# RWKV-7 mixing: the block inverses go from VectorE and GpSimd together to GpSimd alone, in three batches

## The chip, the cores and the metric

The kernel runs on one core of a Trainium2 chip. The metric is the device time of one execution in microseconds; the median of the runs is compared.

## The reference, cut to what matters

The program is one inference step of a four-layer network over 640 tokens (512 latent, 128 context) of width 1024; each layer has a token mixer and an MLP. Layer 2's mixer is a bidirectional RWKV-7 scan, and the change lies there alone:

```python
def wkv7_scan(s0, r, w, k, v, kk, a, reverse):
    def step(s, inp):
        rt, wt, kt, vt, kkt, at = inp
        sa = jnp.einsum('bhvk,bhk->bhv', s, -kkt)
        s = s * wt[:, :, None, :] + sa[..., None] * (kkt * at)[:, :, None, :] + vt[..., None] * kt[:, :, None, :]
        return s, jnp.einsum('bhvk,bhk->bhv', s, rt)
```

The step multiplies the state by (diagonal minus rank one), so a window of 128 tokens can be done at once if a triangular 128x128 matrix is inverted for each window, head and direction. The kernel inverts its 32x32 diagonal blocks directly and gets the rest by matrix products.

## The kernel before

The 16 heads are worked in 8 pairs (KD = 8); T = 640 tokens are NW = 5 windows. The mixer has three stages.

**Preparation** (`prepare(m)` on VectorE, `diagonal`, `spread`, `key_sums`, `bonus` on TensorE, `decays`, `rates`, `exponents`, `take_blocks` on ScalarE). For each pair m and direction d VectorE makes the operands `ar0` and `bt` from `rkv`, `kk`, `e_in` and `e_neg`. SyncE's `rwkv_traffic` stores them in DRAM (`ar_d`, `bk_d`). ScalarE's `take_blocks` copies the 32x32 diagonal blocks out of PSUM and stores them in `blk_d`.

**Inversion.** 8 pairs x 2 directions x 2 heads x 5 windows x 4 = 640 blocks of 32x32, five to a partition. Forward substitution goes through 31 steps; each is a product into `inv_t` and a sum into the rows of the inverse, over (31-j)(j+1) elements a block. VectorE does three blocks of every partition, with the inverse held in PSUM (`inv_p`, which the traces call banks), and GpSimd two, with the inverse in SBUF (`inv_x0`). The input `inv_a` is loaded in two parts (`load_inverse`), the second when the last pair's blocks are stored. ScalarE copies VectorE's result to SBUF, SyncE stores both in `inv_d` and loads them back per pair and direction as `xc`.

**Scan** (`windows(m, d)` on TensorE, `scan_tile` on VectorE and ScalarE). For each pair and direction: `triangles` (masked by VectorE with copy_predicated into `at_`) and `tokens`, then the products `pairs(0)` to `pairs(5)`, of which `pairs(0)` needs `dt_`, the transposed inverse (`turn_inverse`), then states and outputs. `finish(m)` normalises the pair before on VectorE, inside the scan of pair m. SyncE loads the next pair's operands in the same loop.

Each engine runs its own list in order, and semaphores tie the lists. TensorE's first `windows` waits for `inv_copied`, since `inv_p` lies in its banks, and for `b3_landed` (operands) and `masks_landed`. GpSimd's other work is `low_part`, which splits every weight slab (L714); its list is: slabs up to the mixer, its part of the inversion, the other slabs.

Of the kernel before, what the change touches and what calls it, by code (L numbers as in the profile page):

```python
# [11 lines left out]
ALU = mybir.AluOpType  # L12
ACT = mybir.ActivationFunctionType
# [4 lines left out]
P = 128  # L18
D = 1024
KD = D // P  # L20
LAT, CTX = 512, 128
T = LAT + CTX
# [28 lines left out]
PART = ((0, HT - 2), (HT - 2, T))  # L51
INV_N = 5
INV_G = 2
INV_V = INV_N - INV_G

W = 128
NW = T // W
# [21 lines left out]
def build(nc, a, layers=(0, 1, 2, 3)):  # L79
    ctx = ExitStack()  # L80
    with ctx:
# [124 lines left out]
        kk = place("kk", [P, T])  # L206
        blocks = [place("blocks_0", [P, 2 * NW, 32]), place("blocks_1", [P, 2 * NW, 32], at=fs_at)]
        assert cursor[0] <= 229368, cursor[0]

        cursor[0] = hs_at  # L210
        inv_x = [None, place("inv_x1", [P, INV_V, 32, 32])]
        inv_t = [None, place("inv_t1", [P, INV_V * 256])]
        assert cursor[0] <= hs_at + 4 * 2 * 3 * T
        cursor[0] = hs_at + 4 * 2 * 3 * T
        inv_x[0] = place("inv_x0", [P, INV_G, 32, 32])
        inv_t[0] = place("inv_t0", [P, INV_G * 256])
        assert cursor[0] <= hs_at + 4 * 2 * 5 * T

# [6 lines left out]
        inv_at = cursor[0]  # L225
        inv_a = place("inv_a", [P, INV_N, 32, 32])
        assert cursor[0] <= ws_at
        cursor[0] = inv_at
        gt = place("gt", [P, NW, 2, P])
        xc = [place(f"xc_{d}", [P, 2 * NW, 32]) for d in range(2)]  # L230
        assert cursor[0] <= inv_at + 4 * INV_G * 1024
        cursor[0] = inv_at + 4 * INV_G * 1024
        dt_ = place("dt_", [P, 2 * NW, P])
        rhs = place("rhs", [P, NW, 2, 2, HS])
        assert cursor[0] <= ws_at
        tok = place("tok", [P, NW, 3, P], at=ws_at)
# [38 lines left out]
        pu, aux = banks[:, 0:4, :].rearrange("p (t h) n -> p t h n", t=2), banks[:, 4:8, :]  # L275
        inv_p = banks[:, 0:2 * INV_V, :].rearrange("p (q r) (s c) -> p q (r s) c", r=2, c=32)
# [79 lines left out]
        b1_done = sem("b1_done")  # L356
        inv_landed = [sem("inv_landed0"), sem("inv_landed1")]
        inv_done = sem("inv_done")
        inv_copied = sem("inv_copied")
        inv_pool = sem("inv_pool")  # L360
# [98 lines left out]
        def _(sp):  # L459
# [106 lines left out]
            def rwkv_traffic():  # L566

                sp.sem_inc(so_stored, 16)
                for j in range(2):
                    sp.wait_ge(rkv_stored[j], 16 * 2 * KD)  # L570
                inv_parts = blk_d.rearrange("(p n) -> p n", p=P)

                def load_inverse(p, q):

                    for stored in blk_stored:
                        sp.wait_ge(stored, 16 * q * KD // P)
                    sp.dma_start(inv_a[p:q, :, :, :].rearrange("p q r c -> p (q r c)"), inv_parts[p:q, :]
                                 ).then_inc(inv_landed[p > 0], 16)
# [30 lines left out]
                sp.dma_start(vd[:, :], rkv_d[0, 2]).then_inc(v_landed, 16)  # L609
                load_operands(0, 1)  # L610
                sp.dma_start(s0[:, :, :], a["s0"][0]).then_inc(s0_landed, 16)
                sp.dma_start(l2[:, 0, :, :], a["l2"][0]).then_inc(l2_landed, 16)
                inv_all = inv_d.rearrange("(p q n) -> p q n", p=P, q=INV_N)
                for q in range(INV_V):
                    sp.wait_ge(inv_copied, q + 1)
                    sp.dma_start(inv_all[:, INV_G + q, :], inv_x[1][:, q, :, :].rearrange("p r c -> p (r c)")
                                 ).then_inc(x_inv_stored, 16)
                sp.wait_ge(inv_pool, 1)
                sp.dma_start(inv_all[:, 0:INV_G, :], inv_x[0][:, :, :, :].rearrange("p q r c -> p q (r c)")
                             ).then_inc(x_inv_stored, 16)  # L620
                sp.wait_ge(x_inv_stored, 16 * (INV_V + 1))
                for d in range(2):
                    load_inverted(0, d)
                with sp.Fori(0, KD - 1) as m:
                    sp.wait_ge(vrev_ready, m + 1)
# [85 lines left out]
        def _(pool):  # L711
# [15 lines left out]

            def invert_part():

                x, t = inv_x[0][:, :, :, :], inv_t[0]  # L730
                for stored in ab_stored:
                    pool.wait_ge(stored, 32 * (KD - 1))
                pool.wait_ge(inv_landed[0], 16)
# [4 lines left out]
                pool.wait_ge(inv_landed[1], 16)  # L738
                for j in range(31):
                    n, q = 31 - j, INV_G  # L740
                    tj = t[:, 0:q * n * (j + 1)].rearrange("p (q r c) -> p q r c", q=q, r=n)
                    shape = [P, q, n, j + 1]
                    pool.tensor_tensor(tj, inv_a[:, 0:INV_G, j + 1:32, j:j + 1].to_broadcast(shape),
                                       x[:, :, j:j + 1, 0:j + 1].to_broadcast(shape), ALU.mult)
# [14 lines left out]
        def _(pe):  # L759
# [292 lines left out]
            def rwkv():  # L1052
# [185 lines left out]

                pe.wait_ge(inv_copied, INV_V)
                windows(0, 0, None)  # L1240
# [293 lines left out]
        def _(act):  # L1534
# [367 lines left out]
            def rwkv():  # L1902
# [172 lines left out]

                act.wait_ge(inv_done, 1)
                for q in range(INV_V):
                    act.activation(inv_x[1][:, q, :, :], inv_p[:, q, :, :], ACT.Copy).then_inc(inv_copied, 1)

# [172 lines left out]
        def _(dve):  # L2252
# [388 lines left out]
            def rwkv():  # L2641
# [131 lines left out]

                dve.memset(inv_p[:, :, :, :], 0.0)
                dve.drain()
                dve.memset(inv_p.rearrange("p q r c -> p q (r c)")[:, :, 0:1024:33], 1.0)
                dve.drain()
                for landed in inv_landed:
                    dve.wait_ge(landed, 16)
                for j in range(31):  # L2780
                    n = 31 - j
                    t = inv_t[1][:, 0:INV_V * n * (j + 1)].rearrange("p (q r c) -> p q r c", q=INV_V, r=n)
                    shape = [P, INV_V, n, j + 1]
                    dve.tensor_tensor(t, inv_a[:, INV_G:INV_N, j + 1:32, j:j + 1].to_broadcast(shape),
                                      inv_p[:, :, j:j + 1, 0:j + 1].to_broadcast(shape), ALU.mult)
                    dve.drain()
                    rows = inv_p[:, :, j + 1:32, 0:j + 1]
                    op = dve.tensor_tensor(rows, rows, t, ALU.add)
                    if j == 30:
                        op.then_inc(inv_done, 1)  # L2790
                    dve.drain()
# [552 lines left out]
```

## Time and profile before

| | |
|---|---|
| median of 3 runs | 3784.49 us (3779.83 to 3784.79) |
| profiled execution | 3781.54 us, span 3779.7 us |
| TensorE clock granted, mean | 0.968 |
| busy: PE, DVE, ACT, POOL | 92%, 54%, 35%, 34% |

PE is TensorE, DVE VectorE, ACT ScalarE, POOL GpSimd, SPq the queue in which SyncE issues DMAs. TensorE is busy nearly throughout; the 40 slices of the profile show two shallow stretches in the second half of layer 2's work, of which the mixer's preparation and inversion (1640 to 1850 us from the start) are the one that the change touches. Busy shares over the whole span say little about it: it is read from the order of events there.

### The profile page before, as it was taken

The page shows a single profiled execution, that of the slowest core. Times are in us where ns is not written, and L with a number is a line of the kernel's source. Part 1 is how long each engine was busy: PE and PEld are TensorE (multiplying, and loading weights), DVE is VectorE, ACT ScalarE, POOL GpSimd, SP SyncE. Part 2 cuts the span into 40 slices and gives each one's busy share as a digit, 9 for nine tenths or more (in the row PEclk, how much of TensorE's full clock was granted, in tenths as well). Part 3 has the DMA queues.
Part 4 walks back from the last instruction along what each step waited for, and adds up shares of the span by engine and source line. Part 5 has one row for each costly group of instructions (what it writes and reads, how often), then busy time and mean ns, then how long its engine had stood idle before and what let it go on. Part 6 is the DMA issues. An engine that isn't in the chain of part 4 may idle for free.

```text
span 3779.7 us, 67539 instructions
## 1 busy us (share of the span) xinstructions
PE 3473.6 (92%) x25106; PEld 3208.7 (85%) x25106; DVE 2045.8 (54%) x3535; ACT 1332.4 (35%) x2292; POOL 1295.5 (34%) x577
## 2 busy tenths in 40 slices
PE   6899999999999988974599999899999899999998
PEld 3789999998999977962488888799998776899997
DVE  7643774664266558478677676444754554331113
ACT  3343224415422255375232333343224323442223
POOL 0454334635633344301400000464335310464334
PEclk9999999999999999985799999999999999999999
DMA  7544554424455433466111111344544310343223
GB/s 268 157 127 149 195 186 142 131 83 122 133 173 176 149 107 119 143 205 217 52 56 59 43 56 35 112 127 155 185 151 134 98 34 1 101 134 95 72 72 119
DMA packets 174099, 460.36 MB, mean 122 GB/s; under 512 B 56864, under 2 KB 66528, under 8 KB 173152
## 3 DMA queue, kind: packets, MB, share of 16 engines
q1 hardware_dynamic: 145408, 438.46, 36.6%
q10 hardware_dynamic: 28512, 19.45, 1.6%
q8 instruction: 120, 1.97, 0.2%
q14 instruction: 59, 0.48, 0.0%
HBM read 419.41 MB, written 38.44 MB: 121 GB/s over the span
## 4 chain that ended last, share of the span: by engine, by line
issue 73%; POOL 16%; PE 6%; POOLq 2%; ACT 2%; DMA 1%; DVE 0%; ACTq 0%; DVEq 0%; SPq 0%
POOL ws L714 16%; PE banks L787 2%; PE banks L808 1%; PE banks L792 1%; POOLq L750 1%; POOLq L745 1%; PE banks L1117 1%; PE banks L818 0%; POOLq L722 0%; PE banks L1087 0%; PE banks L1140 0%; DMA inv_a<-blk_d 0%; ACT bt L2007 0%; DMA l<-in_l 0%; ACT L1997 0%
## 5 line engine op out<-in xcount | busy, mean ns | idle before, releaser
L714 POOL TENSOR_TENSOR ws<-wr,ws 128x1024 fp32r<-128x1024 f32 x509 | 1240.1, 2437 | 2309.6 <-ACT ws L1550 2309.3
L1550 ACT ACTIVATE ws<-wr 128x1024 fp32r<-128x1024 f32 x509 | 538.2, 1057 | 1053.6 <-PE banks L792 441.2
L787 PE MATMUL banks<-hs,ws 128*128 128x320 f32 x3712 | 564.3, 309 | 0.3 <-DVE hs L2678 0.3
L787 PEld LDWEIGHTS banks<-hs,ws 128*128 128x128 f32 x3712 | 549.3, 188 | 1.2 <-DVE hs L2678 0.9
L808 PE MATMUL banks<-hs,ws 128*128 128x320 f32 (+2 forms) x2624 | 444.9, 320 | 43.4 <-DVE hs L2316 13.7
L808 PEld LDWEIGHTS banks<-hs,ws 128*128 128x128 f32 x2624 | 403.3, 193 | 71.6 <-issue 26.2
L808 PE MATMUL banks<-fs,ws 128*128 128x320 f32 x2304 | 374.2, 312 | 12.9 <-DVE fs L3075 6.8
L2457 DVE SCALAR_TENSOR_TENSOR mjunk<-mr,banks 128x1024 f32<-128x1024 f32 x284 | 335.6, 1219 | 71.7 <-DMA mr<-in_m_slabs 48.4
L808 PEld LDWEIGHTS banks<-fs,ws 128*128 128x128 f32 x2304 | 344.1, 188 | 31.3 <-issue 12.7
L787 PE MATMUL banks<-fs,ws 128*128 128x320 f32 x2304 | 350.1, 309 | 0.0
L787 PEld LDWEIGHTS banks<-fs,ws 128*128 128x128 f32 x2304 | 340.7, 188 | 1.9 <-issue 1.9
L792 PE MATMUL banks<-hs,ws 128*128 128x320 f32 x1856 | 291.0, 309 | 0.0
L792 PEld LDWEIGHTS banks<-hs,ws 128*128 128x128 f32 x1856 | 277.0, 188 | 0.0
L818 PE MATMUL banks<-hs,ws 128*128 128x320 f32 (+2 forms) x1312 | 231.5, 318 | 1.5 <-POOL ws L714 1.5
L2178 ACT ACTIVATE relu<-banks 128x640 f32<-128x640 f32 x92 | 64.9, 706 | 426.9 <-PE banks L792 426.9
L818 PEld LDWEIGHTS banks<-hs,ws 128*128 128x128 f32 x1312 | 205.1, 194 | 11.1 <-issue 6.3
L818 PE MATMUL banks<-fs,ws 128*128 128x320 f32 x1152 | 195.2, 310 | 0.0
L792 PE MATMUL banks<-fs,ws 128*128 128x320 f32 x1152 | 180.6, 309 | 0.0
L818 PEld LDWEIGHTS banks<-fs,ws 128*128 128x128 f32 x1152 | 174.6, 188 | 3.3 <-POOL ws L714 2.1
L792 PEld LDWEIGHTS banks<-fs,ws 128*128 128x128 f32 x1152 | 171.9, 188 | 0.0
L3110 DVE TENSOR_TENSOR acc<-banks,acc 128x640 f32 x64 | 52.8, 824 | 156.4 <-PE banks L792 156.3
L2098 ACT ACTIVATE rhs<-banks 128x128 f32<-128x128 f32 x80 | 22.3, 279 | 310.2 <-PE banks L1268 310.2
(328 smaller groups left out, 4536.4 us busy)
## 6 DMA issues: line engine op xcount, KB each, us to landing
wr<-in_w_slabs SPq DMA_DIRECT2D x509, 512.0 KB, 3.6
mr<-in_m_slabs SPq DMA_DIRECT2D x167, 512.0 KB, 5.0
ar_d<-ar SPq DMA_DIRECT2D x16, 640.0 KB, 3.8
bk_d<-bt SPq DMA_DIRECT2D x16, 640.0 KB, 5.2
ar<-ar_d SPq DMA_DIRECT2D x16, 640.0 KB, 4.0
bk<-bk_d SPq DMA_DIRECT2D x16, 640.0 KB, 5.3
mx<-in_m_slabs SPq DMA_DIRECT2D x16, 512.0 KB, 6.6
rkv<-rkv_d SPq DMA_DIRECT2D x24, 320.0 KB, 5.2
```

Of the source, the lines that this page charges most:

```text
L714: pool.tensor_tensor(ws[s % 2][:, 1, :], wr[:, s % 2, :], ws[s % 2][:, 0, :].bitcast(F32), ALU.subtract).then_inc(lo_ready, 1)
L745: pool.drain()
L750: pool.drain()
L787: pe.matmul(pu[:, t % 2, h, 0:HT], ws[s % 2][:, 0, k * P:(k + 1) * P], src[:, k, part, h * HT:(h + 1) * HT], start=(k + part == 0), stop=F ...
L792: mm = pe.matmul(pu[:, t % 2, h, 0:HT], ws[s % 2][:, 1, k * P:(k + 1) * P], src[:, k, 0, h * HT:(h + 1) * HT], start=False, stop=(k == KD ...
L808: pe.matmul(pu[:, t % 2, h, 0:q - p], ws[s % 2][:, 0, k * P:(k + 1) * P], src[:, k, c, p:q], start=(k + c == 0), stop=False)
L818: mm = pe.matmul(pu[:, t % 2, h, 0:q - p], ws[s % 2][:, 1, k * P:(k + 1) * P], src[:, k, 0, p:q], start=False, stop=(k == KD - 1))
L1117: mm = pe.matmul(gates_at(m)[d][:, h, 0:HT], l2[rows, m % 2, c, :], src[rows, h * HT:(h + 1) * HT], start=True, stop=True, skip_group_chec ...
L1550: act.activation(ws[s % 2][:, 0, :], wr[:, s % 2, :], ACT.Copy).then_inc(hi_ready, 1)
L2178: act.activation(halves(relu[:, j, :]), pu[:, t % 2, :, 0:HT], ACT.Relu).then_inc(relu_ready, 1)
L2457: op = dve.scalar_tensor_tensor(mjunk[:, g, :], at, 0.5, vector[:, g, :], ALU.mult, ALU.mult, accum_out=modt[:, col, g:g + 1].rearrange("p ...
L3110: dve.tensor_tensor(out, pu[:, (t0 + j) % 2, :, 0:HT], out, ALU.add).then_inc(tile_read, 1)
```

## The change

VectorE, ScalarE and PSUM take no part in the inversion any more. GpSimd does all blocks in three batches, two blocks to a partition: pairs 0 and 1 (80 partitions), pairs 2 to 4 (120), pairs 5 to 7 (120). The first batch is loaded by SyncE at the start of its round m = 3 of the preparation and stored at the start of round m = 7. The second is loaded when the scan's first operands have been issued, and stored at round m = 1 of the scan's loop; the third is loaded there and stored at round m = 2. Operands of direction 0 are loaded only after the first batch is stored, since `bk_0`, `vd` and `vr` share its space. TensorE no longer waits for `inv_copied`. SyncE's loop over the scan is written out.

```diff
-INV_N = 5
 INV_G = 2
-INV_V = INV_N - INV_G
+INV_PAIRS = (0, 2, 5, KD)
@@ SyncE, rwkv_traffic
+                def load_blocks(i, pairs):
                     for stored in blk_stored:
-                        sp.wait_ge(stored, 16 * q * KD // P)
+                        sp.wait_ge(stored, 16 * pairs)
+                    part = batch(blk_d, i)
+                    n = part.shape[0]
+                    sp.dma_start(inv_a[i > 0][0:n, :, :, :].rearrange("p q r c -> p (q r c)"), part).then_inc(inv_landed, 16)
+                def store_inverse(i):
+                    sp.wait_ge(inv_pool, i + 1)
+                    ...
+                    sp.dma_start(part, inv_x[i > 0][0:n, :, :, :].rearrange("p q r c -> p (q r c)")).then_inc(x_inv_stored, 16)
                 for m in range(KD):
+                    if m == 3:
+                        load_blocks(0, INV_PAIRS[1])
                     if m == KD - 1:
-                        load_inverse(0, P - P // KD)
+                        store_inverse(0)
...
-                load_inverse(P - P // KD, P)
...
+                sp.wait_ge(x_inv_stored, 16)
                 load_operands(0, 0)
+                load_inverted(0, 0)
...
+                load_blocks(1, KD)
+                for m in range(KD - 1):
+                    if m == 1:
+                        store_inverse(1)
+                        load_blocks(2, KD)
+                        sp.wait_ge(x_inv_stored, 32)
+                    if m == 2:
+                        store_inverse(2)
+                        sp.wait_ge(x_inv_stored, 48)
@@ GpSimd
+            def invert(i):
+                ...
+                pool.wait_ge(inv_landed, 16 * (i + 1))
+                if i:
+                    pool.wait_ge(x_inv_stored, 16 * i)
                 (memsets and the 31 steps as before, on n partitions)
-            invert_part()
+            for i in range(3):
+                invert(i)
@@ TensorE
-                pe.wait_ge(inv_copied, INV_V)
@@ ScalarE
-                act.wait_ge(inv_done, 1)
-                for q in range(INV_V):
-                    act.activation(inv_x[1][:, q, :, :], inv_p[:, q, :, :], ACT.Copy).then_inc(inv_copied, 1)
@@ VectorE: both memsets of inv_p, the waits and the 31 steps taken out
                 dve.memset(at_[:, :, :, :, :], 0.0)
+                dve.memset(dt_[:, :, :], 0.0)
+                dve.wait_ge(blk_stored[0], 16 * KD)
                 dve.memset(sb_[:, :, :], 0.0)
-                dve.memset(dt_[:, :, :], 0.0)
```

The order of SyncE's DMAs from the end of the preparation (its last `bk_d` store) to the loads of the first inverses, before:

```order
L589 DMA bk_d<-bt_121 128x1280
L577 DMA inv_a<-blk_d 16x5120
L598 DMA mask<-in_mask 128x512
L600 DMA ar_139<-ar_d 128x1280
L602 DMA bk_141<-bk_d 128x1280
L609 DMA vd<-rkv_d 128x640
L600 DMA ar_140<-ar_d 128x1280
L602 DMA bk_142<-bk_d 128x1280
L611 DMA s_159<-in_s 128x128
L612 DMA l_115<-in_l 128x384
L616 DMA inv_d<-inv_x_135 128x1024 x3
L619 DMA inv_d<-inv_x_137 128x2048
```

And of the changed kernel at the same place:

```order
L596 DMA bk_d<-bt_121 128x1280
L604 DMA mask<-in_mask 128x512
L606 DMA ar_141<-ar_d 128x1280
L608 DMA bk_143<-bk_d 128x1280
L612 DMA xc_148<-inv_d 128x10x32
L617 DMA vd<-rkv_d 128x640
L618 DMA s_160<-in_s 128x128
L606 DMA ar_142<-ar_d 128x1280
L608 DMA bk_144<-bk_d 128x1280
L612 DMA xc_149<-inv_d 128x10x32
L621 DMA l_115<-in_l 128x384
L576 DMA inv_a_138<-blk_d 120x2048
```

No load of blocks stands ahead of the mask now, the first inverses (`xc`) are loaded among the operands, and the second batch's blocks come last.

VectorE's list from its last preparation operation to the scan's first masking, before (the inversion's 31 steps are cut to their first; names in brackets are the semaphores waited for):

```order
L2760 TENSOR_TENSOR bt_121<-bt_121,e_neg 128x640
L2774 MEMSET banks 128x3072
L2776 MEMSET banks 128x3x32
L2784 TENSOR_TENSOR inv_t_136<-inv_a,banks 128x93 [waits inv_landed1,inv_landed0]
L2788 TENSOR_TENSOR banks<-banks,inv_t_136 128x3x31
```

And after the change:

```order
L2763 TENSOR_TENSOR bt_121<-bt_121,e_neg 128x640
L2777 MEMSET at__153 128x5120
L2778 MEMSET dt__150 128x1280
L2780 MEMSET sb__155 128x512 [waits blk_stored0]
L2832 COPY_PREDICATED at__153<-mask,banks 128x1024 [waits masks_landed,tri_done]
L2832 COPY_PREDICATED at__153<-mask,banks 128x1024 [waits tri_done] x4
L2817 STREAM_TRANSPOSE dt__150<-xc_148 32x10x32 [waits xc_landed0]
```

Sixty-two operations and two memsets are gone from between the preparation and the masking.

GpSimd's list of the changed kernel where its first batch ends and its second begins:

```order
L749 TENSOR_TENSOR inv_t_137<-inv_a_135,inv_x_136 80x62
L753 TENSOR_TENSOR inv_x_136<-inv_x_136,inv_t_137 80x2x31
L741 MEMSET inv_x_139 120x2048 [waits x_inv_stored,inv_landed]
L743 MEMSET inv_x_139 120x2x32
L749 TENSOR_TENSOR inv_t_140<-inv_a_138,inv_x_139 120x62
L753 TENSOR_TENSOR inv_x_139<-inv_x_139,inv_t_140 120x2x31
```

A batch has the same 62 operations of the same length in elements as GpSimd's one part had before; there are three in a row now, all of them ahead of the next weight slab.

## Rows read from the trace of the kernel before

**Rows 1.** Chain of waits, TensorE alone, 1766 to 1850: total us, times, longest.
```profile
PE banks L1280 <- ACT inv_x L2078: 67.4, 1, 67.4
```

**Rows 2.** Timeline, all engines: start us, duration us, instruction, idle before it.
```profile
1762.10 0.46 SPq L589 DMA_DIRECT2D bk_d<-bt  x1
...
1765.02 1.81 POOL L734 MEMSET inv_x<- 128x2048 f32 x1 [132.40 <-DMA ar_d<-ar]
...
1773.64 0.36 SPq L598 DMA_DIRECT2D mask<-in_mask  x1
...
1774.53 0.42 SPq L602 DMA_DIRECT2D bk<-bk_d  x1
...
1778.31 0.33 POOL L743 TENSOR_TENSOR inv_t<-inv_a,inv_x 128x62 f32<-128x62 f32 x1 [11.16 <-DMA inv_a<-blk_d]
...
1830.25 0.80 PE L1280 MATMUL banks<-bk,ar 64*128 64x128 f32 x4 [67.41 <-ACT inv_x L2078]
...
1834.61 2.49 DVE L2846 COPY_PREDICATED at__152<-mask,banks 128x1024 f32<-128x1024 uint32 x2 [0.21 <-PE banks L1285]
...
1841.04 1.29 DVE L2846 COPY_PREDICATED at__152<-mask,banks 128x1024 f32<-128x1024 uint32 x1 [0.78 <-PE banks L1285]
...
1847.02 2.05 DVE L2831 STREAM_TRANSPOSE dt__149<-xc 32x320 f32<-32x320 f32 x4 [4.68 <-DMA xc<-inv_d]
...
1849.12 4.63 PE L1312 MATMUL banks<-dt__149,at__152 128*128 128x128 f32 x20 [8.24 <-DVE dt__149 L2831]
```

**Rows 3.** Windows: stretch, us, busy PE, PEld, DVE, ACT, POOL, clock, DMA, GB/s.
```profile
1675.00:1692.40 17.40, 11.03 (x210) 7.89 (x210) 16.83 (x22) 15.39 (x27) 0.00 (x0) 0.80 0.74 239
...
1778.00:1841.00 63.00, 9.73 (x80) 7.78 (x80) 55.20 (x69) 6.04 (x13) 53.12 (x62) 0.56 0.19 76
```

**Rows 4.** Groups by line, VectorE, 1640 to 1762: count, busy us, mean ns, idle.
```profile
L2736 DVE SCALAR_TENSOR_TENSOR kk<-rkv,pv,banks 128x640 f32<-128x640 f32 x7 | 6.1, 873 | 0.0
...
L2767 DVE TENSOR_TENSOR acc<-banks,rkv 128x640 f32<-128x640 f32 x7 | 5.5, 779 | 0.0
```

**Rows 5.** Timeline, VectorE and GpSimd, 1617 to 1625, in the preparation of pair 0.
```profile
1619.38 0.82 DVE L2759 TENSOR_TENSOR bt<-bt,e_neg 128x640 f32<-128x640 f32 x1
...
1619.56 2.90 POOL L714 TENSOR_TENSOR ws<-wr,ws 128x1024 fp32r<-128x1024 f32 x1 [5.58 <-ACT ws L1550]
1620.12 3.02 DVE L2760 TENSOR_TENSOR bt<-bt,e_neg 128x640 f32<-128x640 f32 x1
```

**Rows 6.** Lines L2457, L2846, whole span: ns min/median/max, first and last start.
```profile
L2457 DVE SCALAR_TENSOR_TENSOR mjunk<-mr,banks x284: 1215/1220/1223, 130.2 to 2858.1; 128x1024 f32<-128x1024 f32 x142
...
L2457 DVE SCALAR_TENSOR_TENSOR mjunk<-mr,silu x50: 1217/1224/3364, 9.4 to 122.2; 128x1024 f32<-128x1024 f32 x50
...
L2846 DVE COPY_PREDICATED at__152<-mask,banks x80: 1280/1305/1332, 1834.6 to 2348.0; 128x1024 f32<-128x1024 uint32 x80
```

**Rows 7.** Line L714, GpSimd's slab operation, whole span, same columns.
```profile
L714 POOL TENSOR_TENSOR ws<-wr,ws x509: 2343/2412/6407, 95.2 to 3755.6; 128x1024 fp32r<-128x1024 f32 x170
```

**Rows 8.** DMA issues at 1762.1, 1774.5 and 1840.5: KB each, us to landing.
```profile
bk_d<-bt SPq DMA_DIRECT2D x1, 640.0 KB, 9.6
...
bk<-bk_d SPq DMA_DIRECT2D x1, 640.0 KB, 7.5
...
inv_d<-inv_x SPq DMA_DIRECT2D x1, 1024.0 KB, 3.9
```

**Rows 9.** Timeline, SyncE's queue: end of the preparation's round 2, stores of round 6.
```profile
1677.84 0.91 SPq L552 DMA_DIRECT2D rkv<-rkv_d  x1
...
1745.07 1.35 SPq L589 DMA_DIRECT2D bk_d<-bt  x1
```

**Rows 10.** Timeline of the scan: SyncE's last DMA of rounds 0 and 1.
```profile
1921.21 0.34 SPq L638 DMA_DIRECT2D l<-in_l  x1
...
1987.71 0.34 SPq L638 DMA_DIRECT2D l<-in_l  x1
```

**Rows 11.** Timeline, TensorE in the scan of pair 1, behind VectorE's `finish(1)`.
```profile
1926.22 0.66 PE L1312 MATMUL banks<-rp,gt 128*128 128x64 f32 x4 [1.15 <-DVE zz L2868]
```

More of the change, by code:

```diff
@@ L206, in build @@
         kk = place("kk", [P, T])
-        blocks = [place("blocks_0", [P, 2 * NW, 32]), place("blocks_1", [P, 2 * NW, 32], at=fs_at)]
+        blocks = [place("blocks_0", [P, 2 * NW, 32]), place("blocks_1", [P, 2 * NW, 32], at=fs_at + 4 * 76 * P)]
         assert cursor[0] <= 229368, cursor[0]
[L210 to L217, printed above, removed]
+        inv_a, inv_x, inv_t = [], [], []
+        for at in (fs_at + 4 * NW * 4 * P, hs_at + 4 * 3 * 2 * T):
+            cursor[0] = at
+            inv_a.append(place(f"inv_a{len(inv_a)}", [P, INV_G, 32, 32]))
+            inv_x.append(place(f"inv_x{len(inv_x)}", [P, INV_G, 32, 32]))
+            inv_t.append(place(f"inv_t{len(inv_t)}", [P, INV_G * 256]))
+        assert cursor[0] <= hs_at + 4 * 7 * 2 * T
         cursor[0] = fs_at
@@ L225, in build @@
         inv_at = cursor[0]
[L226 to L228 removed]
         gt = place("gt", [P, NW, 2, P])
         xc = [place(f"xc_{d}", [P, 2 * NW, 32]) for d in range(2)]
[L231 to L232 removed]
+        assert cursor[0] <= inv_at + 4 * 2 * 1024
+        cursor[0] = inv_at + 4 * 2 * 1024
         dt_ = place("dt_", [P, 2 * NW, P])
         rhs = place("rhs", [P, NW, 2, 2, HS])
[L235 removed]
+        assert cursor[0] <= fs_at + 4 * 76 * P
         tok = place("tok", [P, NW, 3, P], at=ws_at)
@@ L356, in build @@
         b1_done = sem("b1_done")
[L357 to L359 removed]
+        inv_landed = sem("inv_landed")
         inv_pool = sem("inv_pool")
@@ L606, in load_inverted @@
                     sp.dma_start(xc[d][:, :, :], inv_v[2 * m + d]).then_inc(xc_landed[d], 16)
+                sp.wait_ge(x_inv_stored, 16)
                 load_operands(0, 0)
+                load_inverted(0, 0)
                 sp.dma_start(vd[:, :], rkv_d[0, 2]).then_inc(v_landed, 16)
+                sp.dma_start(s0[:, :, :], a["s0"][0]).then_inc(s0_landed, 16)
                 load_operands(0, 1)
-                sp.dma_start(s0[:, :, :], a["s0"][0]).then_inc(s0_landed, 16)
+                load_inverted(0, 1)
                 sp.dma_start(l2[:, 0, :, :], a["l2"][0]).then_inc(l2_landed, 16)
-                inv_all = inv_d.rearrange("(p q n) -> p q n", p=P, q=INV_N)
-                for q in range(INV_V):
[L615 to L624, printed above, removed]
+                load_blocks(1, KD)
[7 more added lines that the diff above has]
+                        sp.wait_ge(x_inv_stored, 48)
                     sp.wait_ge(vrev_ready, m + 1)
@@ L726, in low_parts @@
                     low_part(s1 - 1)
[L728 to L733, printed above, removed]
+            def invert(i):
+                n, q = 16 * NW * (INV_PAIRS[i + 1] - INV_PAIRS[i]) // INV_G, INV_G
+                x, t, blocks_in = inv_x[i > 0][0:n, :, :, :], inv_t[i > 0][0:n, :], inv_a[i > 0][0:n, :, :, :]
+                pool.wait_ge(inv_landed, 16 * (i + 1))
+                if i:
+                    pool.wait_ge(x_inv_stored, 16 * i)
                 pool.memset(x, 0.0)
@@ L737, in invert_part @@
                 pool.drain()
-                pool.wait_ge(inv_landed[1], 16)
                 for j in range(31):
[L740 to L743, printed above, removed]
+                    r = 31 - j
+                    tj = t[:, 0:q * r * (j + 1)].rearrange("p (q r c) -> p q r c", q=q, r=r)
+                    shape = [n, q, r, j + 1]
+                    pool.tensor_tensor(tj, blocks_in[:, :, j + 1:32, j:j + 1].to_broadcast(shape),
                                        x[:, :, j:j + 1, 0:j + 1].to_broadcast(shape), ALU.mult)
@@ L2074, in rwkv @@
                 take_blocks(KD - 1, 1)
-                act.wait_ge(inv_done, 1)
-                for q in range(INV_V):
-                    act.activation(inv_x[1][:, q, :, :], inv_p[:, q, :, :], ACT.Copy).then_inc(inv_copied, 1)
                 def norm_squares_of(m):
@@ L2772, in rwkv @@
                     prepare(m)
[L2774 to L2791, printed above, removed]
                 dve.memset(at_[:, :, :, :, :], 0.0)
+                dve.memset(dt_[:, :, :], 0.0)
+                dve.wait_ge(blk_stored[0], 16 * KD)
                 dve.memset(sb_[:, :, :], 0.0)
-                dve.memset(dt_[:, :, :], 0.0)
                 dve.drain()
```

11 lines of the change are left out of this document (6 added, 5 removed).

## The prediction

> **What bounds the kernel now.** I read the chain of waits of TensorE first, since it is busy 92% of the span: its one long gap near the change is 67.4 us at the first product of the scan (L1280), ended by ScalarE's copy of the inverse out of PSUM [rows 1]. The timeline then gives the order there. VectorE's last preparation operation ends with the last stores (issued 1762.1), the block load that needs them lands late, both inversions start at 1778.3, the scan's first product runs at 1830.25, and its product with the inverse, L1312, at 1849.12, behind GpSimd's share and the way through DRAM [rows 2]. From 1849.12 on the scan runs its own chain. So what counts is when L1312 can start, against the end of the preparation.
>
> The windows say who sets that end: VectorE is busy 16.83 of 17.4 us, the period of one pair, TensorE 11.03, ScalarE 15.39, GpSimd 0 [rows 3]. The preparation is VectorE's.
>
> **What the change takes out.** Let D be the time that the preparation becomes longer. The last `bk_d` store, issued at 1762.1, lands 9.6 us later, at 1771.7 [rows 2, 8]; behind that SyncE may issue the mask, with no block load in between. From the mask's issue (1773.64) to the landing of `bk_0` (1774.53 + 7.5 = 1782.0) it took 8.4 us [rows 2, 8]. The first product then runs at 1771.7 + 8.4 = 1780.1 + D. VectorE's memsets lie ahead of that. From 1830.25 to the end of the fifth masking (1842.33) were 12.1 us, of which some 2.2 because a memset held VectorE until 1834.61; four transposes add 2.05 [rows 2]. L1312 so starts at 1780.1 + 12.0 + D = 1792.1 + D, where 1849.12 stood. The gain is 57.0 - D, less what the scan loses. `xc` is loaded among the operands and should be there before the masking ends.
>
> **D, the price of the first batch.** Its load follows round 2 of SyncE (1678.8, [rows 9]) and lands some 5 us later, an estimate between the 3.9 and 7.5 us of [rows 8]; after a memset of 1.81 [rows 2] the 62 operations start near 1686.6, in pair 3. [...] Beside the inversion of before this cost VectorE nothing, but there it read one operand from PSUM. In the preparation most of its operations read two SBUF tensors. What happens then stands at 1620.12: a product of 0.82 us beside a slab operation of GpSimd takes 3.02, 2.20 more [rows 5]. GpSimd waited for the operation in progress (2.90 instead of its median 2.41, [rows 7]), then held VectorE for all of its own time but 0.2 us. Line L2457 separates the cases: with `silu` in SBUF as second input one of 50 took 3364 ns instead of 1224, with PSUM as second input none of 284 exceeds 1223; the masking, with one SBUF input, keeps to 1280 to 1332, five of its 80 beside the inversion [rows 6].
>
> So each of the 62 holds VectorE for its time less 0.2: 53.1 - 62 x 0.2 = 40.7 us. Not all of VectorE's time is exposed: per pair L2736 (0.87) and L2767 (0.78), which read PSUM, and some 0.6 us of waits and a tiny reciprocal, 2.3 of 17.4 or 13% [rows 3, 4]. D = 0.87 x 40.7 = 35 us. The bounds: the 0.2 is seen on operations of 2.4 us and may not exist for small ones, then D = 0.87 x 53.1 = 46; below, nothing excludes that the short ones slip between VectorE's, D near 0.
>
> [...]
>
> Does the batch end in time? Each GpSimd operation also waits for VectorE's current one, about 0.4 us for 87% of 62, 22 us; 1686.6 + 62 (1778.31 to 1840.5 before, [rows 2]) + 22 = 1771. Round 7, which waits for it, comes at 1746.4 + 35 = 1781 [rows 9]. It fits by 10 us; the store lands 3.9 later [rows 8].
>
> **Batches two and three.** The second is issued last of the scan's loads, at about 1777 + D. Ten transfers are ahead of it; I put its landing at 1789 + D and its end at 1853 + D. SyncE asks for it after its last DMA of round 0, 1921.5 - 57 = 1864.5 + D [rows 10]. The third then lands near 1870 + D, ends near 1935 + D, and is asked for at 1988.1 - 57 = 1931 + D. SyncE waits 4 us and 4 for the store. Queued behind it are `vd` of pair 3 and then that pair's operands, which wait for an output of pair 2, due some 18 us later (half of the 66.5 us between the two rows less what round 2 has spent): free. Without that cover a microsecond there would be one of TensorE.
>
> VectorE's exposed operations in the scan are few: by the code, in direction 0 of a pair, the copy of `vd`, two scalings, one tiny product, and four of `finish`, eight in all; the products for `zz` and the maskings read PSUM. `finish` is on the path already, by 1.15 us [rows 11]. In the old times the two batches lie at 1848 to 1911 and 1928 to 1993. The end of pair 1's `finish`, just ahead of 1926, falls in the pause; pair 2's, 66.5 later, in the third batch. Eight operations at half of 0.66 each is 2.7; I take 3 us. Bounds: 0, and two pairs with the full 0.66 eight times, 10.6.
>
> **The sum.** 57.0 - 35 - 3 = 19. The profiled execution (span 3779.7, time 3781.54) would come to 3762.5, the median of 3784.5 to 3765.5.
>
> **Rivals.** *No exclusion for these short operations.* D near 0, gain 54 to 57, 3729. For it: GpSimd's operations are a third as long as the one observed. Against: every observation of the pair. 0.10. *Partly*: D between 5 and 25, gain 25 to 49, 3748: 0.12.
>
> *GpSimd keeps VectorE out for longer than it works.* If the lock were kept through the drain between two operations, the batch would hold VectorE for its whole 62.2 us: D = 62, 57 - 62 - 3 = -8, 3792, slower. It decides from D = 54 on. For it: a pause of only 0.15 us between GpSimd's operations. Against: VectorE went on 0.2 us before the end of the slab operation. 0.08. [...]
>
> *The first batch is starved.* If VectorE's unbroken chain kept GpSimd waiting, D would be 0, but most of the batch would run after 1762, round 7 of SyncE would hold the last stores for some 50 us, and L1312 would start near 1845: within 0.2%, 3781. Against: GpSimd got in after one operation at 1619.56. 0.05.
>
> **The numbers.** The forecast with D from 28 to 42 and a scan loss of 0 to 8 has 0.53: its own range is 3757 to 3778. A change of 0.2% (7.6 us) is what a measurement of this kernel can tell from none. Faster: 0.10 + 0.12 + 0.53, and 0.03 of the rule's case, 0.78. Within: the rule's other 0.09 and the starved case, less a little, 0.13. Slower: 0.09. The range leaves out the case with no exclusion and the slow one: 3740 to 3783.
>
> **What would show it.** In the changed kernel's trace: the pair's period in the preparation grows from 17.4 to 28 or so while GpSimd works and falls back after; VectorE's L2763 and like lines have medians near 0.82 but maxima of 1.5 to 2; the last `bk_d` store is near 1797; L1312 of the scan near 1827; GpSimd's gap between batches lies in pair 1. Wrong would be: durations of VectorE untouched (first rival), a preparation that ends after 1816, a wait of SyncE for `inv_pool` that delays the last stores, or pairs of the scan that take over 70 us each.

## The result, and the profile after

The changed kernel takes **3761.98 us** (median of 5 runs, 3759.67 to 3769.98) against 3784.46 (5 runs of the kernel before beside them): a ratio of **0.9949**, 95% interval 0.9934 to 0.9963. The ratio is estimated from all the runs; that of the two medians is 0.9941. By the medians the kernel is 22.5 us faster, by the means of the same runs (3763.48 and 3782.95) 19.5; 19 were forecast. The profiled execution took 3761.98 us, and its page begins:

```profile
span 3760.2 us, 67495 instructions
...
PE 3480.1 (93%) x25106; PEld 3213.0 (85%) x25106; DVE 2037.3 (54%) x3471; ACT 1329.7 (35%) x2289; POOL 1434.9 (38%) x705
```

The span is 19.5 us shorter. The chain of waits of TensorE in the changed kernel, 1640 to 1850 us (total, times, longest), answers to [rows 1]:

```profile
PE banks L1116 <- DVE ta L2752: 36.4, 4, 12.3
...
PE banks L1286 <- DMA bk<-bk_d: 12.8, 1, 12.8
...
PE banks L1318 <- DVE dt__150 L2817: 3.4, 1, 3.4
```

The wait of 67.4 us for the inverse is gone. TensorE now waits 36.4 us for VectorE in the preparation, at a line where it waited 5.0 before, and 12.8 us for the last operands on their way through DRAM. The timeline of the changed kernel, all engines, gives the same places as [rows 2], and operations of GpSimd's first and second batch:

```profile
1707.55 1.35 POOL L749 TENSOR_TENSOR inv_t<-inv_a,inv_x 80x414 f32<-80x414 f32 x1
...
1709.50 1.64 DVE L2761 TENSOR_TENSOR ar<-rkv,e_in 128x640 f32<-128x640 f32 x1
1710.60 1.40 POOL L749 TENSOR_TENSOR inv_t<-inv_a,inv_x 80x440 f32<-80x440 f32 x1
1711.06 1.62 DVE L2762 TENSOR_TENSOR bt<-bt,e_neg 128x640 f32<-128x640 f32 x1
...
1714.34 0.76 DVE L2770 TENSOR_TENSOR acc<-banks,rkv 128x640 f32<-128x640 f32 x1
...
1777.80 0.90 SPq L583 DMA_DIRECT2D inv_d<-inv_x  x1
...
1794.36 0.79 SPq L596 DMA_DIRECT2D bk_d<-bt  x1
1801.06 0.33 SPq L604 DMA_DIRECT2D mask<-in_mask  x1
...
1807.95 0.80 PE L1286 MATMUL banks<-bk,ar 64*128 64x128 f32 x4 [12.84 <-DMA bk<-bk_d]
...
1821.95 3.48 PE L1318 MATMUL banks<-dt__150,at__153 128*128 128x128 f32 x20 [3.44 <-DVE dt__150 L2817]
...
1835.11 0.96 POOL L749 TENSOR_TENSOR inv_t<-inv_a,inv_x 120x414 f32<-120x414 f32 x1
```

The reader is to see two engines that hold each other up. GpSimd's operation on 414 elements takes 0.96 us beside the scan and 1.35 beside the preparation; VectorE's products, 0.82 alone [rows 5], take 1.62 to 1.64; and the one that reads PSUM keeps its 0.76. The last `bk_d` store is issued at 1794.36 instead of 1762.10: **D is 32.3 us** (32.1 when each is counted from the first `bk_d` store of its own run, as below). The product with the inverse (L1318 now) starts at 1821.95 instead of 1849.12, 27.2 us earlier.

The windows of the changed kernel, one pair of the preparation in each (columns as in [rows 3]):

```profile
1693.40:1720.97 27.57, 14.13 (x215) 9.65 (x218) 27.16 (x22) 19.39 (x33) 25.02 (x19) 0.63 0.52 158
1720.97:1752.00 31.03, 14.05 (x210) 9.60 (x210) 30.72 (x21) 15.47 (x26) 28.47 (x19) 0.50 0.42 134
1752.00:1776.90 24.90, 12.60 (x210) 8.57 (x210) 24.50 (x22) 13.86 (x23) 22.20 (x20) 0.60 0.40 139
1776.90:1794.36 17.46, 4.81 (x197) 3.27 (x198) 16.67 (x21) 5.03 (x15) 0.21 (x1) 0.56 0.64 205
```

Pairs 3 to 5 take 10.2, 13.6 and 7.5 us more than the 17.4 of [rows 3], and pair 6, beside which GpSimd has finished, 17.46. VectorE counts as busy throughout (27.16 of 27.57 us in pair 3): the time that it is kept out stands inside its operations.

The scan loses time in one pair only. A round is the time from one last DMA of SyncE's loop to the next, one pair of the scan. SyncE's queue in the timeline of the changed kernel, last DMA of rounds 0 to 3, against [rows 10]:

```profile
1893.34 0.33 SPq L644 DMA_DIRECT2D l<-in_l  x1
...
1959.92 0.33 SPq L644 DMA_DIRECT2D l<-in_l  x1
...
2031.45 0.33 SPq L644 DMA_DIRECT2D l<-in_l  x1
...
2097.95 0.33 SPq L644 DMA_DIRECT2D l<-in_l  x1
```

The rounds are 66.6, **71.5** and 66.5 us; the second batch costs nothing, the third 5.0. Where, VectorE and TensorE show in the same timeline, in pair 1 (between the batches) and in pair 2 (beside the third):

```profile
1887.85 0.48 DVE L2839 COPY vr<-vd 128x640 f32<-128x640 f32 x1
1888.24 0.51 DVE L2844 TENSOR_SCALAR sb__155<-s,ewin 64x64 f32<-64x64 f32 x2
1888.79 0.16 DVE L2846 TENSOR_TENSOR ecm<-ewin 128x3 f32 x1
...
1898.49 0.66 PE L1318 MATMUL banks<-rp,gt 128*128 128x64 f32 x4 [1.17 <-DVE zz L2854]
...
1954.44 0.69 DVE L2839 COPY vr<-vd 128x640 f32<-128x640 f32 x1
...
1955.06 1.17 DVE L2844 TENSOR_SCALAR sb__155<-s,ewin 64x64 f32<-64x64 f32 x2
...
1956.26 0.84 DVE L2846 TENSOR_TENSOR ecm<-ewin 128x3 f32 x1
...
1967.06 1.11 PE L1318 MATMUL banks<-rp,gt 128*128 128x64 f32 x4 [3.15 <-DVE zz L2854]
...
1967.96 7.25 PE L1318 MATMUL banks<-zz,gt 128*128 128x128 f32 x40
```

From the copy to `zz` VectorE needs 2.0 us longer in pair 2, and TensorE waits 3.15 instead of 1.17. The 40 matmuls behind that take 7.25 us, 4.63 in the kernel before, and the first four 1.11 instead of 0.66: 2.0 + 2.6 + 0.45 is the 5.0. The windows of the changed kernel around them show what happened to the clock:

```profile
1957.00:1967.90 10.90, 7.75 (x60) 7.24 (x60) 9.82 (x11) 3.20 (x10) 9.34 (x12) 0.94 0.06 18
1967.96:1975.20 7.24, 7.24 (x42) 7.24 (x43) 3.94 (x11) 0.00 (x0) 2.25 (x6) 0.62 0.46 114
```

The granted clock was 0.62 over those 7.24 us, behind a wait of 3.15 us: 0.50 over the first 3.00 of them and 0.71 over the last 4.20. From 1975.2 to 1985.0 it is 1.00 again, and over the same 40 matmuls of pair 1, behind the wait of 1.17 us, it was 1.00 too.

### The profile page after: what moved, and what is told of

Read it like the earlier page. It is cut to its first block, busy times and chain, and to the rows that moved or that the text cites. A ratio compares the mean times of both kernels' runs of the same rounds, so it can differ in the third digit from the quotient of the medians.

```text
span 3760.2 us, 67495 instructions
## 1 busy us (share of the span) xinstructions
PE 3480.1 (93%) x25106; PEld 3213.0 (85%) x25106; DVE 2037.3 (54%) x3471; ACT 1329.7 (35%) x2289; POOL 1434.9 (38%) x705
## 4 chain that ended last, share of the span: by engine, by line
issue 69%; POOL 16%; PE 7%; DVE 3%; POOLq 2%; DMA 1%; DVEq 1%; ACT 1%; ACTq 0%; SPq 0%
POOL ws L720 16%; PE banks L794 2%; PE banks L815 1%; PE banks L799 1%; PE banks L1318 1%; POOLq L756 1%; POOLq L751 1%; PE banks L825 0%; POOLq L728 0%; PE banks L1094 0%; PE banks L1124 0%; DVE ar L2761 0%; DVE bt L2763 0%; PE banks L1147 0%; DVE ar L2759 0%
## 5 line engine op out<-in xcount | busy, mean ns | idle before, releaser
L815 PEld LDWEIGHTS banks<-fs,ws 128*128 128x128 f32 x2304 | 344.1, 188 | 31.8 <-issue 12.7
```

What stands on the lines that cost most here:

```text
L815: pe.matmul(pu[:, t % 2, h, 0:q - p], ws[s % 2][:, 0, k * P:(k + 1) * P], src[:, k, c, p:q], start=(k + c == 0), stop=False)
```

## The experiments

All are made from the changed kernel. Ratios are to runs of the kernel before that stood beside them: 3782.67 us for c0, e1, e2 and e4, 3786.11 for e3, e5 and e6, 3784.11 for e7, e8 and e9. The start of the preparation shifts by some us from run to run, so D is counted from the run's own first `bk_d` store (1640.77 in the kernel before).

**The changed kernel again**, for the spread.

> The changed kernel once more, as the measure for the other runs of this call. Both theories: 3762 us, within 5; pairs 3 to 6 of the preparation 27 to 31 us each, round 2 of the scan 71.5 us between SyncE's last DMAs against 66.5 of the others. If that 5 us was a chance event of one execution, it is missing here.

Measured: 3761.26 us (3756.86 to 3763.29), ratio 0.9943 (0.9927 to 0.996). D is 32.1, the round of pair 2 71.7 us. Both losses repeat.

**e1: the first batch behind the preparation.** The transfer of the blocks moves behind round 7:

```diff
-                    if m == 3:
-                        load_blocks(0, INV_PAIRS[1])
-                    if m == KD - 1:
-                        store_inverse(0)
...
                 sp.wait_ge(b1_done, KD)
+                load_blocks(0, KD)
                 sp.dma_start(mask[:, :], a["mask"]).then_inc(masks_landed, 16)
+                store_inverse(0)
```

> The first batch's blocks are loaded only when the preparation is over, and the scan's operands after the batch, so that GpSimd is idle in the preparation. Theory (GpSimd's operations keep VectorE out): all pairs of the preparation are back to 17.4 us, its last store is issued at 1762, 32 us sooner, and the 62 operations last 62 us as in the kernel before; the batch with its load, store and the operands behind it stands on the path, so the scan's product with the first inverse comes near 1866 instead of 1822 and the time is about 3762 + 44 = 3806. Rival (the preparation is longer because of the new places of the buffers or the DMA traffic): the pairs stay at 27 to 31 us, and the time is near 3838.

Measured: 3806.04 us (3802.58 to 3807.06), ratio **1.0065** (1.0049 to 1.0082). The last `bk_d` store is at 1762.05, D = 0, and the product with the inverse starts at 1862.7, 13.6 us later than before. TensorE's chain of waits in e1, 1640 to 1900 us:

```profile
PE banks L1284 <- DMA bk<-bk_d: 85.9, 1, 85.9
```

Placing the batch beside the preparation is worth 45 us (3806.04 - 3761.26). Without that the change is a loss. The batch on GpSimd alone ends at 1838.40, about where the shared inversion ended (1840.45), but the first operands use its space and are issued only at 1842.61, behind its store; in the kernel before they had been issued at 1774.5. What GpSimd alone would cost with the operands in a place of their own was not tried.

**e2: the first batch only writes.** Its 62 operations become 62 `memset` of the inverse's own space, two for each step, which read nothing and are somewhat shorter (0.68 us on average instead of 0.86). It leaves out the inverses of pairs 0 and 1.

```diff
+                    if i == 0:
+                        flat = x.rearrange("p q r c -> p (q r c)")[:, 0:2 * q * r * (j + 1)]
+                        pool.memset(flat, 0.0)
+                        pool.drain()
+                        op = pool.memset(flat, 0.0)
...
```

> In the first batch each product and each sum is replaced by a memset of the inverse's own space with twice the elements (the first two pairs' inverses are thus not computed), so GpSimd is busy about as long but reads nothing from SBUF. Theory (the second SBUF input of VectorE and a read of GpSimd exclude each other): VectorE's preparation operations stay at 0.82 us, the last store is issued near 1762, the product with the inverse comes near 1790, the time is about 3762 - 32 = 3730. Rival (any GpSimd operation on SBUF keeps VectorE out, or the time goes to its being busy as such): the pairs are stretched by 8 to 14 us each as in the changed kernel, 3755 to 3762.

Measured: 3727.48 us (3724.63 to 3733.81), ratio **0.9854** (0.9838 to 0.9871). GpSimd's groups by line in e2, 1689 to 1790 us, and, by line over the whole span, VectorE's product that is L2763 in the changed kernel:

```profile
L751 POOL MEMSET inv_x<- 80x124 f32 (+15 forms) x31 | 21.1, 681 | 3.6
L753 POOL MEMSET inv_x<- 80x124 f32 (+15 forms) x31 | 21.1, 681 | 3.6
```

```profile
L2772 DVE TENSOR_TENSOR bt<-bt,e_neg x16: 814/817/2992, 1621.1 to 1763.1; 128x640 f32<-128x640 f32 x16
```

42.2 us of GpSimd's work lie beside the preparation and VectorE's median stays at 817 ns; the maximum of 2992 is the slab operation of [rows 5]. The preparation ends as in the kernel before. So D is not the price of a busy GpSimd, of its queue, its semaphores or SyncE's moved transfers; it is the price of what GpSimd reads. The round of pair 2, beside whose scan the third batch still reads, stays at 71.8.

**e3: the first batch on 16 partitions** instead of 80. It leaves out the inverses of four fifths of the first batch's blocks.

```diff
+                if i == 0:
+                    n, x, t, blocks_in = 16, x[0:16], t[0:16, :], blocks_in[0:16]
```

> The 62 operations of the first batch run on 16 partitions instead of 80 (the other blocks of pairs 0 and 1 stay uninverted). Theory (VectorE is kept out for the time of an operation, whatever it moves): nothing changes, 3761 us, pairs 3 to 6 at 27 to 31 us. Rival (the two share bandwidth, so that a fifth of the data costs a fifth): the preparation is 25 us shorter, 3736 us.

Measured: 3763.54 us (3762.35 to 3765.36), ratio 0.9942 (0.9927 to 0.9957), as the changed kernel. GpSimd and VectorE in e3's timeline:

```profile
1712.10 1.35 POOL L751 TENSOR_TENSOR inv_t<-inv_a,inv_x 16x414 f32<-16x414 f32 x1
...
1715.62 1.62 DVE L2764 TENSOR_TENSOR bt<-bt,e_neg 128x640 f32<-128x640 f32 x1
```

The same 1.35 and 1.62 us: on a fifth of the partitions and bytes neither the time nor the hold is shorter. The elements of a partition do set the time: in the kernel before GpSimd's product took 0.33 us on 62 of them and 0.96 on 414. This batch saved nothing by being thinner; e5 has fewer elements in each partition instead.

**e4: the scan without its two batches.** The second and third do one small `memset` in place of their 31 steps; the inverses of pairs 2 to 7 are left out.

```diff
+                if i:
+                    pool.memset(t[:, 0:1], 0.0).then_inc(inv_pool, 1)
-                for j in range(31):
+                for j in range(0 if i else 31):
```

> The second and third batch keep their loads, memsets and stores but leave out their 31 steps (pairs 2 to 7 are worked with a wrong inverse); the first batch is whole. Theory (GpSimd's third batch holds up finish of pair 1 inside the scan of pair 2, and TensorE's longer pause then costs it clock): all rounds of the scan are 66.5 us, TensorE's wait for zz is 1.15 us in every pair, the time is 5 us less than the changed kernel's, 3757. Rival (the 5 us are SyncE's, which loses time with the loads and stores of blocks, or chance): the round stays at 71.5 us or nothing changes, 3762. A second rival, that both batches slow the whole scan by small delays everywhere, would give more than 8 us.

Measured: 3757.35 us (3750.54 to 3764.0), ratio 0.993 (0.9913 to 0.9946); its interval overlaps that of the changed kernel, so the total alone shows nothing, and the profiled execution was with 3764.0 us the slowest of its four. The trace shows it: the rounds, from 1895.62 over 1962.14 and 2028.65 to 2095.16, are all 66.5 us, and TensorE's chain of waits, 1770 to 2400 us, has the 8.1 us of the kernel before, where the changed kernel has 10.1:

```profile
PE banks L1320 <- DVE zz L2856: 8.1, 7, 1.2
```

**e5: pair 0 alone ahead, in five batches.** What the scan needs first is only pair 0. Its 80 blocks get a partition each instead of sharing one by two (31 steps on up to 256 elements instead of 512), loaded in round 5; pair 1 follows at the start of the scan, pair 2, pairs 3 to 5 and 6 to 7 beside it. The batches have places of their own, so that the first operands are loaded ahead of the first store of an inverse.

```diff
-INV_G = 2
-INV_PAIRS = (0, 2, 5, KD)
+INV_BATCH = ((0, 1, 1), (1, 2, 1), (2, 3, 1), (3, 6, 2), (6, KD, 2))
...
-                    if m == 3:
-                        load_blocks(0, INV_PAIRS[1])
-                    if m == KD - 1:
-                        store_inverse(0)
+                    if m == 5:
+                        load_blocks(0, 1)
...
```

> The first batch is pair 0 alone, one block to a partition, loaded at round 5 of the preparation; pair 1 and pair 2 follow as batches of one block to a partition, then pairs 3 to 5 and 6 and 7 with two, all beside the scan. Theory: a batch of one block has about 62 x 0.22 + 39.5 / 2 = 33 us of work, of which 33 - 62 x 0.2 = 21 reach VectorE, 18 after the 13% that read PSUM, some 15 of them before the preparation ends, where 32 stood: the product with the inverse near 1762 + 15 + 27.6 = 1805 instead of 1822. But the later batches now lie beside finish in the scans of pairs 1, 2 and 3 where one did: up to 5 us each, with the clock's fall, against 5 in all. So 3762 - 17 + 5 to 10 = 3750 to 3755. Rival (SyncE's five stores and their waits, or the inverse of pair 1, come too late): TensorE waits for dt_ in pair 1, and the time is 3760 or more.

Measured: **3745.95 us** (3740.77 to 3747.05), ratio 0.9892 (0.9878 to 0.9906). It is 4 us below the expected range; D is 12.6, where 15 were expected. The scan now loses in three pairs, with rounds of 69.3, 71.6 and 71.7 us. TensorE in e5's timeline, pairs 1 and 2:

```profile
1870.65 0.66 PE L1322 MATMUL banks<-rp,gt 128*128 128x64 f32 x4 [2.34 <-DVE zz L2858]
1871.15 6.26 PE L1322 MATMUL banks<-zz,gt 128*128 128x128 f32 x40
...
1941.39 1.12 PE L1322 MATMUL banks<-rp,gt 128*128 128x64 f32 x4 [3.73 <-DVE zz L2858]
```

In pair 1 the wait is 1.2 us too long and the 40 matmuls behind it take 6.26 instead of 4.63, 1.6 more: together the 2.8 us of that round. The windows of e5 show the clock there, 0.69:

```profile
1870.65:1876.15 5.50, 5.50 (x34) 5.50 (x35) 3.56 (x10) 0.00 (x0) 3.24 (x10) 0.69 0.04 11
```

**e6: e5 with the load one round later and with pauses.** GpSimd waits in three batches, at a fixed step, until `finish` of that pair is through.

```diff
-                    if m == 5:
+                    if m == 6:
                         load_blocks(0, 1)
...
                 for j in range(31):
+                    if i in INV_PAUSE and j == INV_PAUSE[i]:
+                        pool.wait_ge(b3_done, i)
```

> As the one with pair 0 first, but loaded at round 6, so that part of the batch runs when the preparation is over, and with GpSimd's batches 2 to 4 paused inside (before step 18, 19 and 14) until finish of the pair before is done. Theory: some 10 to 11 us of the batch still reach VectorE, the product with the inverse comes near 1762 + 11 + 27.6 = 1801, if the inverse isn't late by then (a few us may be lost so); no round of the scan is longer than 67 us. Together 3762 - 21 - 5 = 3736, up to 3742 if the inverse is late. Rival (what costs in the scan isn't the meeting with finish): the rounds are as long as without the pauses, 3745 to 3752. Second rival: GpSimd's start is too late and the scan waits for the first inverse by more than 10 us, 3750.

Measured: 3742.74 us (3736.85 to 3751.01), ratio 0.9889 (0.9872 to 0.9906), not to be told from e5. D is 6.6, but the inverse is now late: TensorE waits 9.8 us for `dt_`, 3.4 in the changed kernel, so the 6 us won are given back. The pause in the scan of pair 2 came a few us late. VectorE and TensorE in e6's timeline:

```profile
1932.67 0.81 DVE L2843 COPY vr<-vd 128x640 f32<-128x640 f32 x1
...
1933.40 1.34 DVE L2848 TENSOR_SCALAR sb__164<-s,ewin 64x64 f32<-64x64 f32 x2
...
1934.77 1.02 DVE L2850 TENSOR_TENSOR ecm<-ewin 128x3 f32 x1
...
1943.84 0.82 DVE L2811 TENSOR_TENSOR hs<-ta,hs 128x640 f32 x1 [0.17 <-issue]
...
1945.32 1.11 PE L1322 MATMUL banks<-rp,gt 128*128 128x64 f32 x4 [3.20 <-DVE zz L2858]
```

`finish` is undisturbed, the four small operations ahead of the reciprocal are not (0.48, 0.51 for two, 0.16 alone), and that is enough: 3.20 us of waiting, and a round of 71.5. This miss shows which operations carry the loss.

**e9: the changed kernel with one pause**, placed by that, ahead of the copy of pair 2.

```diff
+                    if i == 2 and j == 21:
+                        pool.wait_ge(b3_done, 3)
```

> The changed kernel with one wait more: GpSimd's third batch stops before its step 21, near where VectorE begins the copy of vd in the scan of pair 2, and goes on when finish of pair 1 is done. All the work is done. Theory (the 5 us of that round come from VectorE's operations between the maskings and zz meeting GpSimd's): the round is 66.5 us again, TensorE's wait for zz 1.15 us, the time 3757, 5 us under the changed kernel's 3762. Rival (they come from SyncE's held queue): the batch ends 12 us later, the queue is held longer, and the round stays at 71.5 or grows.

Measured: 3758.47 us (3754.49 to 3762.23), ratio 0.9931 (0.9918 to 0.9945). The round of pair 2 is 66.5 us, TensorE's wait 1.16. The 5 us are won back where they were lost; the totals, 2.8 to 3.5 us apart, would not show it alone.

**e7: e5 with two pauses, placed in the same way.**

```diff
+INV_PAUSE = {3: 21, 4: 13}
```

> Pair 0 first, loaded at round 5, with pauses only in the fourth and fifth batch (before step 21 and 13), placed so that the copy of vd, the scalings and the tiny product ahead of finish are covered too, which the pauses of the run before missed. Theory: of the rounds of the scan only the first is long, by the 2.8 us that the third batch costs it without a pause; the two of 71.6 fall to 66.5, and the time is 3746 - 10 = 3736. Rival (a pause makes a later batch late and the scan waits for it): a round grows and the time stays at 3742 or more.

Measured: **3736.77 us** (3732.96 to 3737.84), ratio **0.9872** (0.9857 to 0.9887), the fastest: 47.3 us below the kernel before, 25 below the changed one, with nothing left out. D is 12.7, the inverse is waited for 3.4 us, and the rounds are 67.9, 66.6 and 68.3 us. GpSimd makes no pause in pair 1. TensorE in e7's timeline there, and in the scan of pair 3:

```profile
1877.78 0.66 PE L1322 MATMUL banks<-rp,gt 128*128 128x64 f32 x4 [2.46 <-DVE zz L2858]
1878.28 4.63 PE L1322 MATMUL banks<-zz,gt 128*128 128x128 f32 x40
...
2057.81 0.49 PE L1290 MATMUL banks<-bk,ar 64*128 64x128 f32 x4 [1.84 <-DMA bk<-bk_d]
```

A wait of 2.46 us, 1.3 too long, costs these 1.3 us, but the matmuls behind it take the usual 4.63. The 1.8 us of the third round are what the rival named, in small: the paused last batch ends at 2047.2, and the operands behind its store are issued only at 2051.8 and come late.

**e8: e7 with the load half a round later**, between the two directions of round 5.

```diff
-                    if m == 5:
-                        load_blocks(0, 1)
...
                     for d in range(2):
+                        if m == 5 and d == 1:
+                            load_blocks(0, 1)
```

> The same with the first load half a round later, between the two directions of round 5. Theory: some 9 us less of the first batch lies beside the preparation, which gives back about 3 us, and the first inverse is just in time: 3733. Rival: the inverse is late by as much and nothing is won, 3736.

Measured: 3739.67 us (3737.53 to 3744.44), ratio 0.9879 (0.9864 to 0.9894): nothing won over e7. D is 9.1, 3.6 less, somewhat more than planned. But the inverse is late by 1.2 us more (a wait of 4.65 instead of 3.44 for `dt_`), and the first round of the scan is 69.4 us instead of 67.9. TensorE in e8's timeline there:

```profile
1880.26 0.66 PE L1322 MATMUL banks<-rp,gt 128*128 128x64 f32 x4 [2.32 <-DVE zz L2858]
1880.76 6.26 PE L1322 MATMUL banks<-zz,gt 128*128 128x128 f32 x40
```

The wait is no longer than in e7, but the 40 matmuls take 1.6 us more: the round is longer by TensorE's clock, which was 0.73 over them, as in e5, and 1.00 in e7. The two together take back most of the 3.6 us won. Why the clock fell here and not in e7 stays open.

## Why the prediction was right

**The gain ahead of D (57.0).** Right in size, in parts that balance. From the last `bk_d` store to the product with the inverse were forecast 1792.1 - 1762.1 = 30.0 us; measured are 1821.95 - 1794.36 = 27.6. The store landed 6.7 us after its issue, by the mask's, not 9.6. The mask to TensorE's first product took 6.9 instead of 8.4. From there to the product with the inverse it took 14.0 instead of 12.0. VectorE and TensorE in the changed kernel's timeline, and two windows of equal work, of the changed kernel and of the kernel before (columns as in [rows 3]):

```profile
1818.68 1.29 DVE L2832 COPY_PREDICATED at__153<-mask,banks 128x1024 f32<-128x1024 uint32 x1 [0.79 <-PE banks L1291]
1819.86 2.04 DVE L2817 STREAM_TRANSPOSE dt__150<-xc 32x320 f32<-32x320 f32 x4
```

```profile
1807.95:1813.61 5.66, 5.66 (x33) 4.42 (x33) 1.68 (x2) 0.66 (x2) 0.00 (x0) 0.55 1.11 372
1830.25:1835.97 5.72, 4.82 (x32) 3.73 (x33) 5.24 (x5) 1.32 (x4) 4.77 (x7) 0.72 0.46 183
```

The transposes took their 2.04 us and waited for nothing, so `xc` was there, as forecast. The fifth masking ended 12.0 us behind the first product, as before, and not 9.9: the 2.2 us that the forecast took off for the memset did not come back. TensorE came to its third window after 5.66 us, 5.72 before. Then VectorE behind its memset had kept it waiting (0.90 us); now it was busy throughout, with a granted clock of 0.55 there instead of 0.72.

**D, 35 forecast, 32.3 measured.** The mechanism is shown by two runs: without the reads D is 0 with the rest in place (e2), and a fifth of the partitions changes nothing (e3). The whole-operation bound of 46 falls, and with it the *rule's case* of the numbers (0.03 and 0.09), which is that bound and which no run shows. A product takes 0.80 to 0.82 us more beside GpSimd's operations of 0.96 and 1.02: what is held is their length less some 0.2, for short operations too. Beside the batch 50 of VectorE's operations are over 0.15 us longer than the same ones of the kernel before, by 32.9 us in all. That is 0.66 each, the 0.86 of a GpSimd operation less 0.2. What was off was the share that is exposed: 50 of 62 is 0.81, not 0.87. VectorE's product with two SBUF inputs takes 1.62 us beside GpSimd's operations that read SBUF (the changed kernel) and 817 ns beside those that only write (e2). Beside the inversion of before, with one operand in PSUM, its steps lost nothing: on 621 and 660 elements they took 0.80 to 0.85 us, where the preparation's products on 640, with GpSimd idle, take 0.82 with both inputs in SBUF and 0.78 with one in PSUM. The 53.1 us of GpSimd's work in the forecast are those of [rows 3], on 128 partitions, where the batch has 80. The traces bear that out: its first product took 0.33 us on 128 partitions [rows 2] and 0.32 on 80 (at 1688.21 in the changed kernel), that on 414 elements 0.96 on 128 (before) and 0.96 on 120 (changed).

**The rivals.** No exclusion and partly: D would have been below 25. Kept out for longer: above 54. Neither, by 32.3. *Starved* is refuted by its own place: GpSimd's 62 operations took 80.2 us, 75.7 of them in the three pairs, where they had taken 53.1; it was slowed but got in between VectorE's operations.

**Whether the batch ends in time.** Forecast 1771 against 1781 for round 7. It ended at 1777.11, and SyncE came to the store at 1777.80, behind a `bk_d` store issued at 1777.32. It fitted, but with 0.2 us to the last `bk_d` issue ahead of it, not 10; a few steps more and SyncE would have held the last stores back. Some of GpSimd's operations reach 2174 ns, which the 0.4 us each for VectorE's current operation did not allow for.

**Batches two and three.** End of the second: 1853 + 32.3 = 1885.3, measured 1884.66. End of the third: 1967.3, measured 1970.9; its load landed 10.7 us after its issue instead of some 5. Both within the cover.

**The scan, 3 forecast, 5.0 measured.** The place was right, pair 2 alone; the eight operations lost 2.0 us where 2.7 were estimated. The term that was missing is TensorE's clock behind the longer pause, 0.62 over 40 matmuls instead of 1.00: another 3.0 us. With it the pair takes over 70 us, which the prediction had named as a sign of being wrong for pairs of the scan; it holds for this pair alone. It was expected that the products of `finish` would carry the loss; the small operations ahead of the reciprocal carry 1.6 of the 2.0 us (VectorE's start of it is 2.59 us behind that of the copy instead of 1.02). e4 and e9 show that the third batch at these operations is the cause.

**The sum.** 57.0 - 35 - 3 = 19 was forecast for the span. Measured: 27.2 earlier at the product, 5.1 lost in the rounds behind the first, 0.7 won in the first round (71.4 us from that product to its end instead of 72.1, since the 20 matmuls behind the shorter wait, 3.44 us instead of 8.24, take 3.48 instead of 4.63, at a clock of 0.69 instead of 0.50). That is 22.8 at the last round of the scan (2297.49 instead of 2320.27), and 19.5 at the end. The 3.3 us between lie behind the scan, with the same instructions. A wait of TensorE for `hs` at the scan's end has 1.4 of them (5.07 us instead of 3.65); over the other kernels it is 2.2 to 5.1. What sets it stays open, and runs of one kernel spread by as much. So that 19 comes so near to 19.5 is in part luck: the gain ahead of D was forecast 2.4 too low, D 2.7 too high and the loss of the scan 2.0 too low, and the 0.7 of the first round and the 3.3 behind the scan were not in the sum.

## What to carry to other kernels

Before work goes to GpSimd beside VectorE, sort VectorE's operations of that stretch by where their inputs lie. In these runs those with two SBUF inputs paid almost the whole length of a GpSimd operation that reads SBUF (0.80 to 0.82 us of 0.96 and 1.02), and those that read PSUM nothing (0.76 instead of 0.78). One SBUF input did not decide it: the copy of `vd` (0.69 and 0.81 us instead of 0.48) and the scalings of the state (1.17 and 1.34 for two instead of 0.51) were held too, the reciprocal (4.14 beside the third batch and without it) and the transposes (0.50) were not. Then give GpSimd ahead of time only what the next stage needs at once, with few elements in a partition (pair 0 alone, one block to each of 80 partitions: D from 32.3 to 12.6 us), and pause it where VectorE's short operations stand on TensorE's path, but not for so long that a later batch is late (1.8 us in e7). A single-run trace shows the 3 to 5 us of such a pause, which totals that spread by 5 to 10 us hide.

## What was not expected of the hardware

- A tiny operation waited as long as a large one, which lost 0.80 to 0.82 us: VectorE's product on 128x3 elements took 0.84 and 1.02 us instead of 0.16, and two scalings of 64x64 1.17 and 1.34 instead of 0.51. The scalings of the same size that read PSUM kept their 0.27 to 0.29 beside the second and third batch, the transposes their 0.50, and the masking, with a mask in SBUF, was at most 0.05 us longer than its longest without them (1.38 instead of 1.33).
- GpSimd pays too: beside VectorE's unbroken chain its operations on 414 elements took 1.35 us instead of 0.96, and the longest, on 494, 2.17.
- The length of TensorE's pause alone did not tell what the clock did behind it. Pauses of 3.15 to 3.94 us in the scan were followed by a clock of 0.62 to 0.68 over the next 40 matmuls and rounds of 71.5 to 71.9 us, and one of 3.11 (e3) by 0.73 and a round of 70.1. Pauses of 2.34 (e5) and 2.32 (e8) were followed by 0.73 too, with rounds of 69.3 and 69.4. Behind one of 2.46 (e7) and those of 1.2 the 40 matmuls took their 4.63 us, at 1.00. Three of the five us lost in pair 2 so stood in nobody's waits.
- GpSimd's product on 414 elements takes the same 1.35 us on 80 partitions and on 16.
